# Strassen block products for the up projections of two FFNs and an MLP, in a kernel that runs unit by unit

## The reference

```
x = x + 0.5 * (silu(h @ Wg) * (h @ Wu)) @ Wd       # FFN 1 and FFN 2, h = rmsnorm(x) * g, width 2816
x = x + square(relu(h @ Wup)) @ Wdn                # MLP, h = rmsnorm(x) * g, width 4096
```

## Time and profile before

| | us |
|---|---|
| median of three runs (1830.59 to 1830.64) | 1830.62 |
| the profiled execution | 1830.98 |
| its span, from the first to the last instruction | 1829.2 |
| TensorE busy | 1820.8 (100% of the span) |
| VectorE busy | 966.1 (53%) |
| ScalarE busy | 622.8 (34%) |
| matmul instructions | 8364 |
| HBM read, mean rate | 170.70 MB, 94 GB/s |

### The profile page before, as it was taken

The page is one execution under the profiler, slowest core; times in us unless marked ns, Lnnn a source line. Parts: engine busy times, 40 slices in busy tenths (PEclk is TensorE's granted clock), DMA queues, the critical chain, the costliest instruction groups (busy, mean ns, idle before and its releaser), DMA issues.

```text
span 1829.2 us, 20361 instructions
## 1 busy us (share of the span) xinstructions
PE 1820.8 (100%) x8364; PEld 1501.1 (82%) x8364; DVE 966.1 (53%) x1277; ACT 622.8 (34%) x890; POOL 37.7 (2%) x37
## 2 busy tenths in 40 slices
PE   9999999999999999999999999999999999999998
PEld 7888888878888888888888888888877788888887
DVE  6534434547765534545544443455687664535354
ACT  6312313344332223423422222244655432222133
POOL 0000000000000000000000000000122000000000
PEclk9999999999999999999999999999999999999999
DMA  5332232332122322323233233233421233233332
GB/s 174 105 98 98 93 104 87 90 110 84 55 93 92 104 93 93 103 92 104 92 94 103 93 101 95 94 87 123 143 67 58 81 93 103 93 104 93 104 92 70
DMA packets 52381, 176.22 MB, mean 96 GB/s; under 512 B 6449, under 2 KB 7729, under 8 KB 52289
## 3 DMA queue, kind: packets, MB, share of 16 engines
q1 hardware_dynamic: 50448, 171.60, 29.8%
q10 hardware_dynamic: 1424, 2.14, 0.3%
q0 software_dynamic: 416, 1.18, 0.2%
HBM read 170.70 MB, written 2.10 MB: 94 GB/s over the span
## 4 chain that ended last, share of the span: by engine, by line
PE 98%; DVE 1%; ACT 0%; issue 0%; DMA 0%; ACTq 0%; DVEq 0%
PE ps L1431 29%; PE ps L1433 29%; PE ps L1432 29%; PE ps L1453 2%; PE ps L1455 2%; PE ps L1454 2%; PE ps L1755 0%; PE ps L1766 0%; PE ps L1780 0%; PE ps L1627 0%; PE ps L1463 0%; PE ps L1630 0%; PE ps L1615 0%; PE ps L1475 0%; PE ps L1735 0%
## 5 line engine op out<-in xcount | busy, mean ns | idle before, releaser
L1431 PE MATMUL ps<-Hhi,wh 128*128 128x512 f32 x1520 | 599.2, 394 | 0.0
L1432 PE MATMUL ps<-Hlo,wh 128*128 128x512 f32 x1520 | 591.8, 389 | 0.0
L1433 PE MATMUL ps<-Hhi,wl 128*128 128x512 f32 x1520 | 591.7, 389 | 0.0
L797 DVE TENSOR_TENSOR wl<-raw,wh 128x1024 fp32r<-128x1024 f32 (+1 forms) x318 | 386.4, 1216 | 130.0 <-ACT wh L384 128.2
L384 ACT ACTIVATE wh<-raw 128x1024 fp32r<-128x1024 f32 (+1 forms) x318 | 330.3, 1039 | 321.9 <-PE ps L1433 298.8
L1431 PEld LDWEIGHTS ps<-Hhi,wh 128*128 128x128 f32 x1520 | 285.3, 188 | 64.3 <-issue 5.1
L1432 PEld LDWEIGHTS ps<-Hlo,wh 128*128 128x128 f32 x1520 | 285.4, 188 | 60.9 <-issue 2.6
L1433 PEld LDWEIGHTS ps<-Hhi,wl 128*128 128x128 f32 x1520 | 285.3, 188 | 60.1
L1431 PE MATMUL ps<-Ahi,wh 128*128 128x512 f32 x792 | 308.3, 389 | 0.9 <-DVE Alo L1270 0.6
L1433 PE MATMUL ps<-Ahi,wl 128*128 128x512 f32 x792 | 308.1, 389 | 0.0
L1432 PE MATMUL ps<-Alo,wh 128*128 128x512 f32 x792 | 308.1, 389 | 0.0
(11 more groups left out here) (268 smaller groups left out, 1230.6 us busy)
## 6 DMA issues: line engine op xcount, KB each, us to landing
raw<-in_w_gu SPq DMA_DIRECT2D x86, 512.0 KB, 3.3
raw<-in_w_d SPq DMA_DIRECT2D x32, 512.0 KB, 3.5
raw<-in_w_up SPq DMA_DIRECT2D x32, 512.0 KB, 3.3
raw<-in_w_dn SPq DMA_DIRECT2D x32, 512.0 KB, 3.9
raw<-in_w_d SPq DMA_DIRECT2D x16, 384.0 KB, 3.1
raw<-in_w_v SPq DMA_DIRECT2D x8, 512.0 KB, 4.0
raw<-in_w_cc SPq DMA_DIRECT2D x8, 512.0 KB, 3.4
raw<-in_w_cu SPq DMA_DIRECT2D x8, 512.0 KB, 3.4
```

The lines of the kernel that those rows point to most:

```text
L797: dve.tensor_tensor(WL[u % 3][:, 0:n], RAW[u % 3][:, 0:n], f32(WH[u % 3][:, 0:n]), ALU.subtract).then_inc(s["wl"], 1)
L1431: pe.matmul(ps, wh[:, c], hi[:, k, :], start=(k == 0), stop=False)
L1432: pe.matmul(ps, wh[:, c], lo[:, k, :], start=False, stop=False)
L1433: last = pe.matmul(ps, wl[:, c], hi[:, k, :], start=False, stop=(k == nb - 1))
```

## The change

**Pairs.** Units u and u+1 of an FFN for j >= 5 (FFN 1) or j >= 4 (FFN 2), and up units 2i and 2i+1 of the MLP in groups 1 to 3, become a pair. A pair multiplies a 2x2 grid of weights (two output blocks of 128 by two halves of the 1024 features) by a 2x2 grid of activations (two halves of the features by two halves of 256 tokens) with Strassen's scheme: seven block products instead of eight. FFN 1 has 17 pairs, FFN 2 has 18, the MLP 12.

- TensorE (`pair`): 7 products c = 0 to 6, each of 4 blocks by 3 matmuls of 256 columns. They use three banks: products 0, 2, 4, 6 add up in one, 1 and 5 in another, 3 in the third. Product 2 waits until ScalarE has copied product 0 out of its bank (`tap`), product 4 for the tap of product 2, product 6 for `merge` 1, which VectorE does after product 4.
- VectorE: 4 sums of raw weight halves (`total`), 7 `pair_lo` of 512 columns, 3 `merge` of 256 columns, and per FFN pair two half products and one `a_lo`, per MLP pair two `a_lo`.
- ScalarE: 7 `pair_hi` of 512 columns, 3 taps of 256 columns; per FFN pair silu and high part; per MLP pair relu, relu, square, relu, square and two squares into Ahi.
- SyncE: 4 DMAs of 256 KB instead of 2 of 512 KB. The buffers raw, wh and wl become rings of six halves.

**Operands.** The right sides of the seven products (`BThi`, `BTlo`) are built once per layer, with R multiplied in, in four steps kp of two feature blocks each: VectorE makes the seven sums in `BF` (`operands`: six instructions, four of 256 columns, each but two behind a wait for the one before), ScalarE copies all 7x256 columns to BThi, VectorE subtracts them to BTlo (`operands_lo`). Tables give the place of each step: key 2j stands between the gate and `feed(u+3)` of column pair j, key 2j+1 at j's end; in the MLP the key is the unit.

The two `operands` below are those of ScalarE and the subtraction of VectorE; `pair` is TensorE's.

```diff
+JS = (5, 4)
+    BUILD = [{2: 0, 4: 1, 6: 2, 7: 3}, {1: 0, 3: 1, 4: 2, 6: 3}, {2: 0, 4: 1, 6: 2, 8: 3}]
+    BUILT = [{3: 0, 5: 1, 7: 2, 8: 3}, {2: 0, 4: 1, 5: 2, 7: 3}, {3: 0, 5: 1, 7: 2, 9: 3}]
...
+        def operands(i, kp):
+            act.wait_ge(s["bf"], 4 * i + kp + 1)
+            act.activation(BThi[:, :, kp, :], BF[:, 0:NP, :], ACT.Copy).then_inc(s["bh"], 1)
...
+        def operands_lo(i, kp):
+            dve.wait_ge(s["bh"], 4 * i + kp + 1)
+            dve.tensor_tensor(BTlo[:, :, kp, :], BF[:, 0:NP, :], f32(BThi[:, :, kp, :]),
+                              ALU.subtract).then_inc(s["bl"], 1)
...
+        def pair(p):
+            if PREVP[p] is None or layer(PREVP[p]) < layer(p):
+                pe.wait_ge(s["bl"], 4 * layer(p) + 4)
+            for c, b in enumerate((0, 1, 0, 2, 0, 1, 0)):
+                pe.wait_ge(s["wl"], WN[p][c])
+                if c in (0, 1, 3):
+                    pe.wait_ge(s[FREE[p][b][0]], FREE[p][b][1])
+                elif c in (2, 4):
+                    pe.wait_ge(s["tp"], 3 * PAIR[p] + c - 1)
+                elif c == 6:
+                    pe.wait_ge(s["ev"], EV0[p] + 2)
+                ps = BK[BANK[p][b]][:, LEFT]
+                whi, wlo = WHP[WS[p][c]], WLP[WS[p][c]]
+                new = c in (0, 1, 3)
+                for kp in range(4):
+                    w = slice(kp * P, kp * P + P)
+                    pe.matmul(ps, whi[:, w], BThi[:, c, kp, :], start=(new and kp == 0), stop=False,
+                              skip_group_check=not new)
+                    pe.matmul(ps, whi[:, w], BTlo[:, c, kp, :], start=False, stop=False, skip_group_check=not new)
+                    last = pe.matmul(ps, wlo[:, w], BThi[:, c, kp, :], start=False, stop=(kp == 3),
+                                     skip_group_check=not new)
+                last.then_inc(s["pe"], 1)
```

More of the change, by code:

```diff
@@ L116, in _units, with _counts, bank, slot @@
         for j in range(8):
-            add("w_up", 8 * g + j, 0, 8, 7)
+            add("w_up", 8 * g + j, 0, 8, 7, g > 0 and j % 2 == 0)
         for n in range(KT):
             add("w_dn", n, 8 * g, 8 * g + 8, 7)
-    before, at, done = {}, 0, 0
+    return plan
+def _counts(plan):
+    bank_free, slot_free, raw_free, raw_count = {}, {}, {}, [0] * 6
+    at = done = pe = w = ws = rs = squared = 0
+    last = None
+    def bank(banks):
+        nonlocal at
+        b = at % banks
+        at += 1
+        return b
+    def slot(pe_done):
+        nonlocal ws
+        i = ws % 6
+        ws += 1
+        free = slot_free.get(i)
+        slot_free[i] = pe_done
+        return i, free
+    def raw(wl_done, n):
+        nonlocal rs
+        i = rs % 6
+        free = max(raw_free.get(i + j, 0) for j in range(n))
+        for j in range(n):
+            raw_free[i + j] = wl_done
+        rs += n
+        raw_count[i] += 16
+        return i, raw_count[i], free
@@ L139 @@
-NU = len(UNITS)
+        pe += 1
+        PEN.append(pe)
+        if ws % 2:
+            slot(slot_free.get(ws % 6))
+        i, free = slot(pe)
+        free = max(free or 0, slot(pe)[1] or 0)
+        WS.append(i)
+        WF.append(free)
+        if u < 2:
+            WN.append(0)
+            RSL.append(2 * u)
+            RN.append(0)
+            RF.append(0)
+            rs += 2
+            continue
+        w += 1
+        WN.append(w)
+        i, c, free = raw(w, 2)
+        RSL.append(i)
@@ L726, in act_program, with high, second_left, second_square @@
             square(n)
+        def high(j, r):
+            act.activation(Ahi[:, j, :], TA[r], ACT.Square).then_inc(s["ah"], 1)
+        def second_left(p):
+            act.wait_ge(s["pe"], PEN[p][6])
+            act.activation(TA[5][:, LEFT], BK[BANK[p][0]][:, LEFT], ACT.Relu).then_inc(s["tz"], 1)
+        def second_square(p):
+            act.wait_ge(s["tz"], PAIR[p] - PAIR[MLP_UP[1]] + 1)
+            own.wait()
+            act.activation(TA[7], TA[5], ACT.Square)
         for g in range(4):
@@ new lines, in total @@
+        def total(p, i):
+            b21, b11, b22, b12 = (RAWP[r] for r in RSL[p])
+            s1, s2, s3, s4 = sums_of(p)
+            a, b, op = ((b21, b22, ALU.add), (s1, b11, ALU.subtract), (b11, b21, ALU.subtract),
+                        (b12, s2, ALU.subtract))[i]
+            for r in ((0, 2), (1,), (), (3,))[i]:
+                dve.wait_ge(s[f"raw{RSL[p][r]}"], RN[p][r])
+            if PREVP[p] is not None:
+                dve.wait_ge(s["wl"], WN[PREVP[p]][(1, 2, 4, 5)[i]])
+            if i == 3 and layer(p) == 2:
+                dve.wait_ge(s["bl"], 12)
+            if i in (1, 3):
+                dve.wait_ge(s["sd"], 4 * PAIR[p] + i)
+            dve.tensor_tensor((s1, s2, s3, s4)[i], a, b, op).then_inc(s["sd"], 1)
@@ L1489, in ffn @@
                     u = GU[f, g] + 2 * (j - a)
-                    if f == 0 and j == 0:
+                    if u in PAIR:
+                        pair(u)
+                    elif f == 0 and j == 0:
                         first_units()
```

458 lines of the change are left out of this document (377 added, 81 removed), and 2 rows, old and new, of the table SEMS.

## The result

The changed kernel takes 1864.25 us (median of 4 runs, 1862.97 to 1866.03), the one before 1830.63: a ratio of 1.018 (95% interval 1.017 to 1.020), slower by 34 us. The forecast was 1866.5.

A forecast was written before the change was run, and what follows sets the result against it. TensorE, busy 100% of the span, was taken to bound the kernel. 1831.0 - 28.0 (FFN pairs) + 0.3 (MLP pairs) + 24.2 + 23.2 + 13.0 (building) + 3 (clock) = 1866.7 us, stated as 1866.5; range 1848 to 1884.

The forecast's parts named there:

- Building: Building operands at layer starts makes TensorE wait: 24.2 us in FFN 1, 23.2 in FFN 2, 13.0 in the MLP.
- The circle laid out as 14.3 us: VectorE and ScalarE work in series per two units while operands are built: 14.3 us against TensorE's 10.88.
- Prices: Instruction times in a building step: BTlo 2.04 us and sums 3.0 us on VectorE, BThi 1.68 us on ScalarE.
- FFN pairs: 35 pairs in the FFNs gain 0.80 us each, 28.0 us, with all of TensorE's handshakes in time.
- 84 matmuls x 0.120 = 10.08: TensorE's time for a pair in us, from 256-column matmuls 0.120 us apart, in place of 10.88.
- MLP pairs: 12 pairs in the MLP gain nothing: +0.3 us for three groups, between -3 and +5.
- a length of 11.2 us: MLP pair's circle through ScalarE and VectorE, via lo 6 to merge 2: 11.2 us, over 10.08 and 10.88.
- The term of 3: TensorE's lower clock behind the waits of 14.2 and 7.5 us: 3 us taken, between 0 and 10.2.
- The rival: After each long wait TensorE runs at 1.2 GHz for about a unit: +7 us more, 1874; chance 30%.
- each product pays 0.08 us at its border: Two waits at each product's start break TensorE's stream, 329 times: +26 us, 1890; chance 6%.
- Covered, faster: Every building step fits into the slack of two units, so waits of 60.4 us vanish: 1804 us; chance 9%.
- point of decision: Building is covered if the circle of 14.3 us falls under 10.88, or waits below half (28 of 60).

The follow-up runs named there:

- experiment 6: Changed kernel with only the MLP pairs reordered: ScalarE's hi 5 and hi 6 earlier, VectorE's first a_lo behind lo 6; 1863.60 us (1.018).
- experiment 7: As experiment 6, plus ScalarE's hi 0 of the next pair before the second Square, VectorE's merge 1 before the second a_lo; 1859.66 us (1.016).
- experiment 9: Changed kernel plus 33 and 57 matmuls with no use before TensorE's two FFN waits for BTlo; 1862.67 us (1.018).
- Experiment 4: Changed kernel with no pairs in the FFNs' first groups, ScalarE's weights' split before BThi's copy, FFN building steps moved later; 1818.63 us (0.993).
- experiment 5: As Experiment 4, but ScalarE's order as in the changed kernel, BThi's copy ahead of the weights' split; 1837.32 us (1.004).
- experiment 8: Changed kernel plus 24 and 46 matmuls with no use before TensorE's two FFN waits for BTlo; 1864.82 us (1.019).

## Why the prediction was right

Verdict and time were right, the time within 2.3 us; some of its terms were not, and part of that cancelled. By the ledger the pairs gave 8.2 us more than forecast, and the building with its clock cost 4.2 us more (67.6 for 63.4), so that the time came out this close partly by luck.

- **Building.** Right in place and nearly in size. The circle laid out as 14.3 us was 14.10. Prices: BTlo 2.02 us for 2.04, BThi 1.70 for 1.68, the six sums 3.12 for 3.0. FFN 1: 4.79, 0.63, 2.90, 7.55 and 0.97 for 4.8, 3.5, 3.1, 9.0 and 3.5; FFN 2: 0.51, 2.93, 3.69, 12.78 for 0.5, 3.1, 5.4, 14.2. The waits came out shorter than forecast at unit 7 and at the first pair because TensorE reached them late, at a lower clock: start times agree (unit 7 at 53.7 for 54.1, the pair at 82.5 for 83), and these set the end. With the gains of the pairs inside taken out (3 and 4 of 0.98), group 0 costs 25.1 and 26.0 us in the FFNs, for 24.2 and 23.2; the clock is in the measured ones. MLP: 16.5 for 13.0; its waits were 0.7, 4.0 and 6.9, 11.7 together, and behind the last two came some 3 us more at the lower clock.
- **FFN pairs.** Mis-sized: the step "84 matmuls x 0.120 = 10.08". A pair of after takes 9.90 us. In group 0 of FFN 1 the first and last start below have 105 distances of 0.118 between them:

```profile
99.52 0.28 PE L1921 MATMUL ps<-BThi,wl 128*128 128x256 f32 x1
...
111.89 0.28 PE L1921 MATMUL ps<-BThi,wl 128*128 128x256 f32 x1
```

  The 0.120 of the earlier trace rows came from products near the end of the kernel that are built otherwise; what makes them 2 ns slower stays open. A pair gains 0.98 us, not 0.80, which is 6 us more in 35 pairs. That no handshake waits in the FFNs was right; in a group of six 0.5 us of 5.9 went elsewhere.
- **MLP pairs.** The forecast, +0.3, was near the measured -2.6, in its range. The step that failed is which circle: a length of 11.2 us was laid out through lo 6, 10.79 was measured, and moving lo 6 forward did not shorten it (experiment 6). With hi 0 of the next pair and merge 1 moved forward it fell to 9.94 (experiment 7).
- **Clock.** The term of 3 was right in size. Behind the wait of 12.78, sixteen matmuls stood 0.21 apart and not 0.118, 1.6 us with the first two (1.7 by experiment 9); behind that of 6.91 ten of 512 columns at 0.43 for 0.227, 2.1 us. The rival had the mechanism and not the price: the level did fall to 0.50 behind most waits, long and short, and where that lay on the path it cost some 2 us each time, not a unit's 5.1. The Trainium skill, TensorE: Matmul & The Clock Gate, Part 1, says that an idle array falls back to 1.2 GHz until it has been busy again. The traces agree behind the waits named here, but not behind every one (3.37 us in experiment 9). TensorE's busy time fell by 24 us and not by the forecast 37, though a pair gains more: in after 86 matmuls stand apart as at the lower clock, 13 us more together than at the higher one.
- **Rivals.** That each product pays 0.08 us at its border is ruled out by 105 even distances, over eight borders. "Covered, faster" was wrong for this kernel, but its point of decision was named wrongly too: I wrote that it would take BTlo and BThi at half their price. Experiment 4 shows that at the same prices, with no pairs in the first group, other places and ScalarE's copy behind the split, all of it is covered in the FFNs; experiment 5 shows that without the last of these it is not.

## What to carry to other kernels

Work added to half-idle engines is paid for by the chain that it stands in, not by their busy share: lay out the circle from one use of the bound engine to the next, and put long new instructions behind those that feed it, and where slack has come back. Where a large gain is eaten by a fixed cost at the start, read the ledger of a marker that both kernels have, group by group, before giving up on the idea: here seven pairs fewer, building steps at other places and a new order of instructions on ScalarE and VectorE turned +34 us into -32. When a new order does not shorten a pitch, look for what the second engine still waits for before concluding that it is full.

## What the hardware showed that was not expected

The granted clock fell after idle times as short as 1.9 and 2.4 us (experiment 8), while behind the 0.97 us at 88.96 in after it was full. It also stayed full behind 3.37 us in experiment 9 and behind 2.88 us before unit 9 of FFN 1 in experiment 7, where in after it fell behind 2.90 us at the same place. So the length of the idle time alone does not tell whether the clock falls; what decides stays open. Matmuls of 256 columns ran 0.118 us apart in the pairs and 0.120 in other products of the same shape, so that, beside 0.227 us for 512 columns, an estimate gives some 9 ns that are fixed per matmul, and not 13.
